# Last mixer: all weight low parts made on VectorE instead of mostly on GpSimd

## The reference

```python
h = rmsnorm(x, norm_mix_w)
proj = h @ w_in                              # 1024 x 3080, the first product
qkv, z, b_logit, a_logit, lru_x, lru_gate = split(proj)
qkv = silu(causal_depthwise_conv(qkv))       # 4 taps
o = gated_delta_rule_chunked(l2norm(q), l2norm(k), v, g, beta)   # the rule
gdn_out = rmsnorm(o, gdn_norm_w) * silu(z)   # 512 wide
xr = causal_depthwise_conv(lru_x) + bias
lru_out = rg_lru(xr) * gelu(lru_gate)        # 512 wide
x = x + concat([gdn_out, lru_out]) @ w_out   # 1024 x 1024
m = rmsnorm(x, norm_mlp_w)
x = x + relu(m @ w_ff1) ** 2 @ w_ff2
```

## Time and profile before

| | |
|---|---|
| median of 3 runs | 1141.92 us (1139.85 to 1142.61) |
| profiled execution | 1138.88 us |
| its span, first to last instruction | 1137.1 us |
| mean granted TensorE clock | 0.982 of full speed |
| busy: PE / DVE / ACT / POOL | 1087.8 / 735.5 / 579.1 / 388.1 us |
| low parts on DVE (L1703) | 146, 289.9 us |
| low parts on POOL (L2381) | 41, 183.8 us |

### The profile page before, as it was taken

How to read it: one execution, slowest core, us unless ns; L and a number is a source line. 1 busy time by engine, 2 the same in 40 slices (tenths; PEclk the granted TensorE clock), 3 DMA queues, 4 the chain that set the end, 5 groups by cost and what they waited for, 6 DMA issues and landing times.

```text
span 1137.1 us, 20145 instructions
## 1 busy us (share of the span) xinstructions
PE 1087.8 (96%) x8424; PEld 1023.1 (90%) x8424; DVE 735.5 (65%) x1177; ACT 579.1 (51%) x797; POOL 388.1 (34%) x236
## 2 busy tenths in 40 slices
PE   7999999999999999999999999996998889999997
PEld 6999988998999999998899899996887768999996
DVE  4752258777677764225877767767874778666674
ACT  4555466554445635546554445567336645344442
POOL 1386654221122356665513012344432135101021
PEclk9999999999999999999999999988998999999999
DMA  7753444555744664443554664463221245564741
GB/s 241 226 182 127 146 136 148 186 167 177 229 155 147 223 200 149 149 149 111 180 168 156 200 223 157 142 204 111 77 75 38 64 159 186 168 211 135 233 139 60
DMA packets 173577, 180.11 MB, mean 158 GB/s; under 512 B 4272, under 2 KB 171568, under 8 KB 173360
## 3 DMA queue, kind: packets, MB, share of 16 engines
q1 hardware_dynamic: 173488, 178.84, 49.0%
HBM read 177.78 MB, written 1.05 MB: 157 GB/s over the span
## 4 chain that ended last, share of the span: by engine, by line
PE 66%; issue 12%; DVE 10%; ACT 8%; POOL 4%; DMA 1%; SPq 0%; DVEq 0%; POOLq 0%; ACTq 0%
PE psum L650 65%; DVE sb_scratch L1694 3%; ACT sb_w_hi L1213 3%; ACT sb_scratch L1213 2%; DVE sb_w_lo L1703 2%; POOL sb_scratch L2410 1%; POOL sb_scratch L2429 1%; ACT L1213 1%; DVE sb_rs L1745 1%; PE psum L842 1%; DMA sb_scratch<-in_x 1%; ACT sb_sq L1213 0%; POOL sb_rs L2397 0%; POOL sb_scratch L2418 0%; DVE sb_xt L1718 0%
## 5 line engine op out<-in xcount | busy, mean ns | idle before, releaser
L650 PE MATMUL psum<-sb_xg_hi,sb_w_hi 128*128 128x256 f32 x1632 | 470.4, 288 | 4.0 <-issue 1.8
L650 PE MATMUL psum<-sb_xg_lo,sb_w_hi 128*128 128x256 f32 x1632 | 463.6, 284 | 0.0
L650 PE MATMUL psum<-sb_xg_hi,sb_w_lo 128*128 128x256 f32 x1632 | 463.5, 284 | 0.0
L1213 ACT ACTIVATE sb_w_hi<-sb_raw 128x2048 fp32r<-128x2048 f32 (+4 forms) x187 | 316.3, 1698 | 157.6 <-PE psum L650 95.7
L1703 DVE TENSOR_TENSOR sb_w_lo<-sb_raw,sb_w_hi 128x2048 fp32r<-128x2048 f32 (+4 forms) x146 | 289.9, 1990 | 122.2 <-ACT sb_w_hi L1213 122.1
L650 PEld LDWEIGHTS psum<-sb_xg_hi,sb_w_hi 128*128 128x128 f32 x1632 | 314.8, 193 | 9.0 <-issue 4.7
L650 PE MATMUL psum<-sb_hid_both,sb_w_hi 128*128 128x512 f32 (+1 forms) x928 | 309.4, 385 | 10.4 <-DVE sb_hid_both L1771 6.3
L650 PEld LDWEIGHTS psum<-sb_xg_lo,sb_w_hi 128*128 128x128 f32 x1632 | 315.0, 193 | 0.3
L650 PEld LDWEIGHTS psum<-sb_xg_hi,sb_w_lo 128*128 128x128 f32 x1632 | 314.9, 193 | 0.0
L2381 POOL TENSOR_TENSOR sb_w_lo<-sb_raw,sb_w_hi 128x2048 fp32r<-128x2048 f32 (+1 forms) x41 | 183.8, 4486 | 191.7 <-ACT sb_w_hi L1213 191.7
L650 PE MATMUL psum<-sb_hid_both,sb_w_lo 128*128 128x256 f32 x864 | 243.1, 281 | 0.0
(11 more groups left out here) (159 smaller groups left out, 992.5 us busy)
## 6 DMA issues: line engine op xcount, KB each, us to landing
sb_raw<-in_w_in SPq DMA_DIRECT2D x52, 1024.0 KB, 5.2
sb_raw<-in_w_up SPq DMA_DIRECT2D x44, 1024.0 KB, 5.1
sb_raw<-in_w_ff SPq DMA_DIRECT2D x16, 1024.0 KB, 5.6
sb_raw<-in_w_down SPq DMA_DIRECT2D x16, 768.0 KB, 4.4
sb_raw<-in_w_down SPq DMA_DIRECT2D x16, 640.0 KB, 4.2
sb_raw<-in_w_ff SPq DMA_DIRECT2D x16, 640.0 KB, 4.3
sb_raw<-in_w_out SPq DMA_DIRECT2D x8, 1024.0 KB, 5.0
sb_raw<-in_w_ff SPq DMA_DIRECT2D x8, 768.0 KB, 4.5
```

The costliest lines, as they stand in the source:

```text
L650: return nc.tensor.matmul(ps, lhsT, rhs, start=start, stop=stop, skip_group_check=True)
L1213: return nc.scalar.activation(out_, in_, func, **kw)
```

## The change

The entry for the stage (2, "in") and that for (2, "out", "gdn") are taken out of the table. The table has no other entry for these stages, so the lows of slabs 2, 3 and 5 to 12 of the first product and of slabs 0 to 2 of the rule's output product get the name `split_lo` and are made by VectorE at the place where its queue already has the call. GpSimd still makes the low of slab 2 of the feed-forward stage (2, "up", 0) and those of the two layers before. Nothing else differs: the instructions on TensorE, ScalarE and SP are the same, but the waits of TensorE and SP on these lows are on the other semaphore.

```diff
-POOL_SLABS = {(2, "in"): (2, 3, *range(5, 13)), (2, "out", "gdn"): range(3), (2, "up", 0): (2,)}
+POOL_SLABS = {(2, "up", 0): (2,)}
 for _l in range(DEPTH):
     POOL_SLABS.update({(_l, "in"): (2, *range(11, 20)), (_l, "proj"): (0, 1), (_l, "out"): (2,), (_l, "up", 0): (2,)})
 POOL_SLABS[(0, "in")] = range(11, 20)
```

## The result

The median goes from 1141.92 us to 1125.49 (four runs, 1122.83 to 1126.93): ratio 0.9856, 95% interval 0.9834 to 0.9879, so 16.4 us less. The profiled execution took 1122.83 against 1138.88.

What follows compares the result with a forecast made beforehand. TensorE sets the end, so only its idle spells pay, lengthened where GpSimd's lows stall VectorE's SBUF operations. Idle -8.7 and clock -1.7 make -10.4: from 1141.92 to 1131.5 us, range 1126.5 to 1139.

Steps and rivals of the forecast that it cites:

- Slab 2: First product: its low on VectorE takes the place of the stall in the norm's square root; 0.
- Slab 3: Its low delays slab 1's convolution inputs and ScalarE's table loads by 1.1; TensorE's 0.89 us spell at 778.01 grows by 1.1.
- Slab 5: Convolution at 778.96 loses its 4.2 us stall, the low is covered by ScalarE; key sums 3.0 us earlier.
- Slab 6: Stall of 3.8 goes, key products give back 1.1, bare low costs 2.3; spell at 809.89 totals -3.4 us.
- slab 7: Its 2.3 us low stands before the level 1 masks, leaving TensorE a spell of 0.5; total -2.9 us.
- Slabs 9, 10 and 11: Convolutions without stalls remove TensorE's spells of 1.59, 0.79, 1.22 and 2.12 us; running total -4.5, -6.5, then -8.6.
- Rival A: Stalls go but VectorE's added lows release TensorE about as late as now: -3 up to slab 7, 1139 us; chance 0.18.
- Output product: Lows 0 and 1 (2.4 us) delay the residual additions before 922.16; the spell of 4.00 stays: -0.1 us.
- The clock: With shorter TensorE spells, one stretch at the lower clock less: -1.7 us, from 0 to about -8.5.
- Rival C: Clock stays at its upper level through most of the mixer: -14 to -17 us, 1126 us; chance 0.15.
- B: VectorE becomes the bound, added lows stand bare before what TensorE waits for: +12.5 us, 1154 us; chance 0.05.
- D: VectorE's queue lacks the call for some of the 13 slabs, so the change doesn't do what it says; given nothing.

Runs made afterwards that it cites:

- 3: Changed kernel plus 13 extra GpSimd subtractions of a spare tile, which read SBUF and whose result nobody uses: 1151.67 us, ratio 1.0100 to the kernel before.
- 4: Changed kernel plus 13 extra GpSimd memsets of a spare tile, which only write: 1123.96 us, ratio 0.9860 to the kernel before.
- 10: Changed kernel with GpSimd's other 28 lows moved to VectorE too: 1123.42 us, ratio 0.9851 to the kernel before.
- 11: Changed kernel run once more, unchanged: 1125.14 us, ratio 0.9856 to the kernel before.
- 1: Changed kernel with the output product's three half lows back on GpSimd: 1124.88 us, ratio 0.9873 to the kernel before.
- 5: Kernel before with only the lows of slabs 5 and 6 moved to VectorE: 1134.22 us, ratio 0.9939.
- 6: Kernel before with only the lows of slabs 7 to 12 moved to VectorE: 1131.16 us, ratio 0.9909.
- 9: Kernel before plus 37 idle TensorE transposes ahead of the work ending four spells (838 to 869 us): 1143.59 us, ratio 1.0014.
- 8: Changed kernel with VectorE's lows of slabs 3 and 4 made one place later: 1122.68 us, ratio 0.9838 to the kernel before.
- kernel 2: Kernel before with only the output product's three half lows moved to VectorE: 1137.2 us, ratio 0.9992.

## Why the prediction was wrong where it was, by its own steps

- **What bounds the kernel, and the stall: right, and shown.** TensorE waits for none of these low parts; GpSimd's reading holds VectorE up. Taken away, VectorE is fast; put back with no data flow at all (3), it stands again; with a writing operation in its place (4) it doesn't.
- **Slab 2, 0.** Its low (756.79 to 759.07) puts off the norm's square root by 1.1, and this, no longer held, ends at 760.77 where it ended at 762.05. TensorE has other work there (0.23 idle before the product at 765.80); nothing to speak of.
- **Slab 3, 1.1 late.** The spell grew by 2.1, not by 1.1. It ends at 778.22 where it ended at 778.01; less the 0.5 of the earlier start that is 0.7 late. The low ends at 768.11, forecast 768.9. The rest is TensorE, which arrived 1.9 earlier (775.23 for 777.12) because 755 to 765 was at 0.90 and 0.76, not 0.74 and 0.66. The step is right; the clock made the spell longer.
- **Slab 5, -3.0; spell 3.7.** The key sums begin 4.0 earlier, 3.5 without the earlier start; the spell is 1.95. TensorE arrived 1.8 later than before because of the spell of 2.99 and the low stretch behind it. In 4, 10 and 11, where the spell before is shorter, it is 3.54, near the forecast.
- **Slab 6, -3.4 for level 1; slab 7, a spell of 0.5.** Spells of 0.38 (forecast 0.7) and 0.46. In idle time level 1 is -4.2 (forecast -3.4), behind slab 7's spell -3.7 (forecast -2.9); with the work level 1 is -6.6. Slab 8, 0: no spell there, as forecast.
- **Slabs 9, 10 and 11: three times right.** Gone are 1.59, 0.79, 1.22 and 2.12. Rival A lived on margins of 0.1 and 0.3 us; they held. VectorE's third-level additions begin at 829.18, right behind the low of 826.98, and its last masks at 853.11, behind the low of 850.79: the order and durations of the replay.
- **Slab 12, and the buffers: 0, right.** No engine waits for a transfer from 750 us on in the mixer, before or after; slab 6's low ends at 801.47, earlier than the 804.5 that was reckoned with; and 873 to the end is as long as before to 0.3 us.
- **Output product, -0.1: too small.** The spell is 4.00 in every trace with these lows on GpSimd (before, 1, 5, 6, 9) and 2.4 to 3.6 in every one with them on VectorE; pairs of traces alike up to there put it at 0.6 (6 and 8) and 1.3 us (1 and the changed kernel). The two lows delay VectorE by less than the step said: it put the four operations on the hidden tiles at 924.0, 3.4 us after TensorE stops; in 8 they begin 2.9 after it (1.6 before) and no longer stand still. In the profiled pair a low stretch at 898 to 903 took the gain back.
- **Sum of the idle time: -8.6 forecast up to 873, -9.4 measured;** with the output product -8.7 and -10.8. VectorE as a whole gained 7.8 us of busy time where some 5 were forecast.
- **The clock, -1.7: this is the step that failed.** The same matmuls gained 6.5 in the profiled pair. I took one low stretch less, with the others as an outer bound of -8.5. Three went (840, 855, 870), and the one behind the long spell got shorter: -1.9, -3.2 and -1.4 in the table, against +1.6 in 778 to 785 behind the grown spell, so -4.9. Another -1.6 lies ahead of 778, where the stretch at 755 to 765 was shorter; it is scatter, as below. Every place where the replay took spells out whole had a low stretch behind it in the profile of before: 835 to 845 (0.95 and 0.71), 855 to 860 and 870 to 875 (0.66 each), 3.4 us at half speed and so 1.7 us each. Taking the stretch out with its spell would have made the term -5.1, the sum -13.8, and the forecast 1128.1. The range failed with it: by the prediction's own bound, all stretches gone (1.7 three times and 3.7 are 8.8, not 8.5), the time could be 1124.7 or less, and the range stopped at 1126.5. How much of the -4.9 the change has caused is not settled by this pair: kernel 2, whose program is unchanged up to the output products, takes 28.6 us from level 3 to the last level's product where before takes 31.1, for no other reason than the clock.
- **Rival C had the place and the size (1126),** with a chance of 0.15. B, D: excluded by the result. So is A: the margins held.

Adding up, -9.4 idle and -4.9 clock are 14.3 of the 16.5 up to 873; the other 2.2 are the 0.5 before the stage and the 1.6 of the stretch at 755 to 765. These are of one pair of executions; over the runs, the mean clock was about 0.981 before and 0.9845 after, and 0.0035 of 1125 us is about 4 us, an estimate that agrees with the size of the term; I can't part them finer. What decides where the clock falls stays open: between 815 and 880 it never fell without a spell ahead, it fell behind some spells and not behind others of the same length, and the two tries at filling them left a spell standing each.

## What to carry to other kernels

Work put on GpSimd to relieve VectorE is not free for VectorE if it reads SBUF: look for VectorE operations with two SBUF operands that last as long as GpSimd's and end with it, and price the move by the stalls less the added work, along the queue, at the places where TensorE stands still. Where TensorE doesn't wait for VectorE, the same move is worth nothing (10). When a replay takes out an idle spell that has a stretch of lower clock behind it, the stretch goes as well in all traces here: count it in, with a range down to nothing, since the same spell stands without a stretch in other executions. Dummy matmuls in its place won nothing here.

## What the runs showed of the hardware that was not expected

- GpSimd's writing operation (128 x 2048 in 1.81 us) leaves VectorE's two-operand operations alone at 483 ns; the subtraction of the same size (4.08 us) brings them to 794 (4 and 3).
- The granted clock is not a function of the program. At 755 to 765, behind a spell of 0.50 that is the same in every kernel, the two windows were 0.90 and 0.76 in the changed kernel and 0.66 and 0.73 in run 11, which is the same program; they were 0.50 and 0.50 in 4 and 9, 0.66 and 0.72 in 2, 0.91 and 0.75 in 3 and 6, 0.95 and 0.71 in 8. Summed over the windows from 750 to 775 (1 less the clock, times 5 us), the traces other than that of 3, which has a spell of its own there, lose 1.7, 3.4 or 6.8 us to within 0.1, and nothing between.
- Nearly all scatter between executions goes with it: over the 47 runs of the kernel before in the three batches, the seven with a mean clock of 0.986 took 1135.6 to 1137.9 us and the nine with 0.976 to 0.978 took 1141.2 to 1145.8. Two traces of one kernel can differ by 5 us for this reason alone.
- Stretches at the lower level stood behind spells as short as 1.22 and 2.12 us in the kernel before, and behind 1.14 in 9; but none stood behind 1.59, 0.79 and 1.21 in 2, nor behind 2.83 in 3.
